# Moving the even steps' transposes in among the value products of an attention kernel, with all transposes in fp32r and one product made narrower

## The reference, cut to what matters

```python
h = _rmsnorm(x, norm_mix_g[l])
a_q, a_k, a_v, b_q, b_k, b_v, c_q, c_k, c_v, c_f, gates = jnp.split(h @ w_in[l], splits, axis=-1)
o_a = _diff_attention(...)           # 4 heads: (softmax(s0) - lam * softmax(s1)) @ v, v 128 wide
o_b = _chunk_band_attention(...)     # 8 heads of 64, own chunk of 64 keys and 8 before it
o_c = _forgetting_attention(...)     # 8 heads of 64, causal, with a cumulative log-forget bias
g = jax.nn.sigmoid(gates)
merged = g0 * (o_a @ w_br_a) + g1 * (o_b @ w_br_b) + g2 * (o_c @ w_br_c)
x = x + merged @ w_out[l]
h = _rmsnorm(x, norm_ffn_g[l])
x = x + (jax.nn.silu(gt) * up) @ w_down[l]
return _rmsnorm(x, final_norm_g)
```

## Time and profile before

| | |
|---|---|
| median of 3 runs | 1815.77 us (1815.49 to 1816.34) |
| profiled execution: time, span | 1817.18 us, 1815.4 us |
| PE busy | 1795.1 us (99% of the span), 9048 matmuls |
| PE weight loads busy | 1507.9 us (83%) |
| DVE, ACT, POOL busy | 1253.9 (69%), 898.9 (50%), 360.6 us (20%) |
| mean granted TensorE clock | 0.999 of full |

### The profile page before, as it was taken

How to read it: one execution, slowest core, us unless ns; L and a number is a source line. 1 busy time by engine, 2 the same in 40 slices (tenths; PEclk the granted TensorE clock), 3 DMA queues, 4 the chain that set the end, 5 groups by cost and what they waited for, 6 DMA issues and landing times. The chain is left out here.

```text
span 1815.4 us, 26104 instructions
## 1 busy us (share of the span) xinstructions
PE 1795.1 (99%) x9048; PEld 1507.9 (83%) x9048; DVE 1253.9 (69%) x2374; ACT 898.9 (50%) x1742; POOL 360.6 (20%) x350
## 2 busy tenths in 40 slices
PE   8999999999999999999999999999999999999998
PEld 6888888888888888888888888888888888888886
DVE  5467766666667775777646778787766877766665
ACT  5555655667666775743424224553333333344445
POOL 2356331212111121013310000003222232200011
PEclk9999999999999999999999999999999999999999
DMA  8526333322332233333336572226566576479522
GB/s 236 161 95 197 92 95 85 72 75 69 94 93 73 65 97 128 131 119 116 129 116 214 175 266 93 116 65 215 196 201 205 174 237 227 160 264 396 195 74 93
DMA packets 195945, 268.01 MB, mean 148 GB/s; under 512 B 9988, under 2 KB 132996, under 8 KB 191864
## 3 DMA queue, kind: packets, MB, share of 16 engines
q1 hardware_dynamic: 191944, 262.07, 43.9%
q0 software_dynamic: 1664, 4.19, 1.6%
q10 hardware_dynamic: 2224, 0.30, 0.1%
HBM read 187.82 MB, written 80.02 MB: 148 GB/s over the span
## 5 line engine op out<-in xcount | busy, mean ns | idle before, releaser
L220 PE MATMUL ps<-h_hi,w_hi 128*128 128x512 f32 x888 | 359.4, 405 | 3.9 <-DVE q_stack L1064 2.4
L222 PE MATMUL ps<-h_hi,w_lo 128*128 128x512 f32 x888 | 347.2, 391 | 0.0
L221 PE MATMUL ps<-h_lo,w_hi 128*128 128x512 f32 x888 | 346.6, 390 | 0.0
L857 POOL TENSOR_TENSOR w_lo<-w_raw,w_hi 128x256 fp32r<-128x256 f32 x148 | 109.7, 772 | 461.4 <-ACT w_hi L925 461.4
L222 PEld LDWEIGHTS ps<-h_hi,w_lo 128*128 128x128 f32 x888 | 166.7, 188 | 37.0
L220 PEld LDWEIGHTS ps<-h_hi,w_hi 128*128 128x128 f32 x888 | 166.5, 188 | 36.3 <-DVE q_stack L1064 3.2
L221 PEld LDWEIGHTS ps<-h_lo,w_hi 128*128 128x128 f32 x888 | 167.1, 188 | 29.1
L1093 DVE CUSTOM_DVE_ANT_0 probs_bc<-ps,bias 128x640 f32<-128x640 f32 (+7 forms) x128 | 90.5, 707 | 73.3 <-PE ps L1275 31.4
L2290 POOL TENSOR_TENSOR bias<-w_raw 128x512 f32<-128x512 f32 x19 | 26.9, 1414 | 521.6 <-DMA w_raw<-in_w_gate_up 509.4
L220 PE MATMUL ps<-down_ring_w,down_ring_a 128*128 128x512 f32 x308 | 119.8, 389 | 0.0
L221 PE MATMUL ps<-down_ring_w,down_ring_a 128*128 128x512 f32 x308 | 119.8, 389 | 0.0
(11 more groups left out here) (365 smaller groups left out, 4391.2 us busy)
## 6 DMA issues: line engine op xcount, KB each, us to landing
w_raw<-in_w_in SPq DMA_DIRECT2D x50, 512.0 KB, 5.3
w_raw<-in_w_gate_up SPq DMA_DIRECT2D x44, 512.0 KB, 4.3
k_stack<-k_stack SPq DMA_DIRECT2D x24, 512.0 KB, 5.4
gate_in<-gates_scratch SPq DMA_DIRECT2D x24, 512.0 KB, 3.7
down_rows<-in_w_down SPq DMA_DIRECT2D x11, 1024.0 KB, 7.0
hidden_scratch<-hidden_stage SPq DMA_DIRECT2D x22, 512.0 KB, 4.9
weight_sums_scratch<-weight_sums SPq DMA_DIRECT2D x11, 1024.0 KB, 4.9
gates_scratch<-gate_sigmoid SPq DMA_DIRECT2D x21, 512.0 KB, 3.1
```

The lines of the kernel that those rows point to most:

```text
L220: nc.tensor.matmul(out, w_hi, x_hi, start=first, stop=False)
L221: nc.tensor.matmul(out, w_hi, x_lo, start=False, stop=False)
L222: return nc.tensor.matmul(out, w_lo, x_hi, start=False, stop=last)
L857: last = nc.gpsimd.tensor_tensor(w_lo[part], w_raw[part], w_hi[part].bitcast(F32), ALU.subtract)
```

## The change

In branches 2 and 3, at even steps from 2 on, the transposes no longer stand as a burst between the scores and the pieces. The pieces come first, and then the products of the group, with one transpose put in after each high product and before its low product; transposes left over follow the last product. Odd steps and step 0 keep their order. In branch 1 the low product is 128 wide and no longer 256. The transposes of lines 535, 1964 and 2952 read their tiles as fp32r against the fp32r identity, and that identity is now made by GpSimd early in the first block and not by DVE later.

```diff
             pool.wait_ge(made, 3)
+            nc.gpsimd.tensor_copy(keep["ident_r"][:, :], ident[:, :]).then_inc(consts, 1)
             nc.gpsimd.memset(wf_both[:, :, :].bitcast(F32), 0.0).then_inc(made, 1)
...
-            dve.wait_ge(made, 3)
-            nc.vector.tensor_copy(keep["ident_r"][:, :], ident[:, :]).then_inc(consts, 1)
...
-                return nc.tensor.transpose(turn_bank(g)[:, j * P:(j + 1) * P],
-                                           x_all[:, 4 * half + j, k * P:(k + 1) * P], ident[:, :])
+                return nc.tensor.transpose(turn_bank(g)[:, j * P:(j + 1) * P].bitcast(F32R),
+                                           x_words[:, 4 * half + j, k * P:(k + 1) * P], keep["ident_r"][:, :])
...
-                        last = nc.tensor.matmul(pv_bank[:, 0:2 * P], pta_lo[:, lc % 4, x * P:(x + 1) * P], v,
+                        last = nc.tensor.matmul(pv_bank[:, 0:P], pta_lo[:, lc % 4, x * P:(x + 1) * P], v[:, 0:P],
                                                 start=False, stop=tile == n - 1)
...
-            def times_v_bc(b, c, g):
+            def times_v_bc(b, c, g, beside=None):
...
+                if beside is not None:
+                    pe.wait_ge(scaled[beside % 2], STEPS // 2 * (c["unit"] - UPB) + (beside // 2 + 1))
+                tiles = tiles_of(b, place_of(b, beside)[0])[1] if beside is not None else 0
...
+                    if tile < tiles:
+                        turn_tile(b, c, beside, tile)
+                        tile += 1
                     nc.tensor.matmul(pv_half(g)[0:HD, lo:hi], v[:, 0:HD], ptb_lo[:, m, k, lo:hi], start=False, stop=False)
                 last = nc.tensor.matmul(pv_half(g)[:, lo:hi], v, ptb_hi[:, m, k, lo:hi], start=False, stop=True)
                 last.then_inc(pv_group, 1)
+                for rest in range(tile, tiles):
+                    turn_tile(b, c, beside, rest)
+
+            def turn_tile(b, c, s, tile):
+                sizes = chunks_of(b, place_of(b, s)[0])
+                j = 0 if tile < sizes[0] else 1
+                lc, x = chunks_through(b, s - 1) + j, tile - sum(sizes[:j])
+                turn = nc.tensor.transpose(turn_bank[lc % 2][:, x * P:(x + 1) * P].bitcast(F32R),
+                                           probs_words[:, s % 3, tile * P:(tile + 1) * P], keep["ident_r"][:, :])
+                if x == sizes[j] - 1:
+                    turn.then_inc(turned, 1)
...
-                    if s in turns:
+                    if b == 0:
+                        if s in turns:
+                            turn_probs(b, c, s)
+                        next_pieces(pieces_at[s])
+                        if s >= 2 and s % 2 == 0:
+                            times_v_a(c, s // 2 - 1)
+                    elif s >= 2 and s % 2 == 0:
+                        next_pieces(pieces_at[s])
+                        times_v_bc(b, c, s // 2 - 1, s if s < STEPS else None)
+                    else:
                         turn_probs(b, c, s)
-                    next_pieces(pieces_at[s])
-                    if s >= 2 and s % 2 == 0:
-                        if b == 0:
-                            times_v_a(c, s // 2 - 1)
-                        else:
-                            times_v_bc(b, c, s // 2 - 1)
+                        next_pieces(pieces_at[s])
...
-                    last = nc.tensor.transpose(turn_view(t)[:, k, :], o_tile[:, t % 2, k * P:(k + 1) * P], ident[:, :])
+                    last = nc.tensor.transpose(turn_view(t)[:, k, :].bitcast(F32R), o_words[:, t % 2, k * P:(k + 1) * P],
+                                               keep["ident_r"][:, :])
...
-                        last = nc.tensor.transpose(turn_bank(g)[:, j * P:(j + 1) * P], normed[:, j, k * P:(k + 1) * P], ident[:, :])
+                        last = nc.tensor.transpose(turn_bank(g)[:, j * P:(j + 1) * P].bitcast(F32R),
+                                                   normed_words[:, j, k * P:(k + 1) * P], keep["ident_r"][:, :])
```

More of the change, by code:

```diff
@@ L233, in block_norm @@
         x_all = sb("x_all", [P, TT, D])
+        x_words = nc.alloc_sbuf_tensor_at("x_words", [P, TT, D], F32R, offset=113152)
         junk = sb("square_out", [P, 4, D])
@@ L592, in _ @@
             pe.wait_ge(scaled, 2)
+            pe.wait_ge(consts, 1)
             for j in range(2):
@@ L1305, in times_v_bc @@
                 close = both[-1] if len(both) > 1 else one[-1]
+                tile = 0
                 for k in [x for x in both + one if x != close] + [close]:
@@ L1441, in block_merge @@
         o_tile = h_hi_room[:, 1, :].rearrange("p (n f) -> p n f", n=2)
+        o_words = also("o_tile_words", [P, 2, BR_W], F32R, 6144)
         o_hi = [o_first_hi, keep["act_hi"], h_hi[:, KH:KT, :]]
@@ L2028, in block_ffn @@
         normed = merged[:, 0:4 * D].rearrange("p (t d) -> p t d", t=4)
+        normed_words = also("normed_words", [P, 4, D], F32R, 112640)
         junk = merged[:, 4 * D:6 * D].rearrange("p (t d) -> p t d", t=2)
```

## The result

The change makes the kernel slower: 1846.49 us in the median of 5 runs (1845.51 to 1847.82), against 1816.07 (1815.49 to 1816.34) before. The ratio is 1.0165, with an interval of 1.0154 to 1.0177. The profiled execution took 1846.5 us with a span of 1844.7, so the two spans differ by 29.3 us. The forecast was 1835, with a range of 1825 to 1845: the direction was right, the size too small and the time outside the range.

What follows compares the result with a forecast made beforehand. PE, busy for 99% of the span, was taken as the bound. Terms +12.7 (branch 2), +9.4 (branch 3), -1.1 and -1.7 sum to +19.3 us on the median of 1815.77, giving 1835 us, range 1825 to 1845.

Steps and rivals of the forecast that it cites:

- a rival with a chance of 0.03: Clock falls to half level for 3 us after eight long waits, each costing 1.5 us more: 1847 us; chance 0.03.
- g3 in branch 2: Steps 8 and 9: late transposes delay ACT's copy, exp and take-out, so PE goes on 2.0 us later per unit.
- g3 in branch 3: Steps 6 and 7: the same late chain costs PE 1.8 us per unit, 0.8 in the last unit.
- g4 in branch 2: Steps 12 and 13: ACT's copy of g4 comes late and PE, which did not wait before, loses 0.75 us per unit.
- Banks at steps 14 and 15: No scores between the two steps, so PE waits for both banks: 0.55 us per unit, 0.6 in branch 3.
- The price of an interleaved transpose: A transpose between a high and a low product costs 0.08 us, bounded by 0.06 and 0.135.
- What the interleaving gains by itself: Gain of 0.4 us per unit of branch 2, only 0.13 of it real, and nothing in branch 3.
- The narrow low product: Branch 1: 144 narrower low products gain between 0 and 8.6 us, taken as 0.0075 each, -1.1 us.
- fp32r: 160 transposes go from 0.109 to 0.085 us each: 4 us gain at most, 0 at least, taken as -1.7.
- the waits don't grow: Rival: ACT and DVE catch up inside the products, only gains are left, 1811.5 us; chance 0.05.
- transposes are dear: Rival: the low product pays like a 128-column load, 0.135 us, +9 us: 1844 and up; chance 0.09.
- only the g3 waits grow: Rival: bank and g4 waits are absorbed, 7 us less, 1828 us, inside the range; no chance of its own.

Runs made afterwards that it cites:

- the earlier take-out: Changed kernel with other take-out steps alone: g2 and g3 at steps 4 and 8 (branch 2), 4 and 6 (branch 3), g4 at 12: 1861.95 us.

## Why the prediction was wrong, and where it was right

**The step that failed is the clock, which the sum puts at nothing.** "Total: +12.7 + 9.4 - 1.1 - 1.7" takes the granted clock of 1.00 of the earlier trace rows as a constant, though it had been read in a stream without waits of 2 us, and leaves the half level to a rival with a chance of 0.03. The runs showed 10.5 us in its place: five stretches of 3.4 us at 0.50 in the branches, 1.5 us each and 7.5 together, at waits for g3 near 2 us, and one of 10.2 us in the first block, 3.0. Filling the waits without shortening them gave 7.4 us back in the seven units. The waits for g3 and their length the working had.

The rival had the mechanism right, in the branches, and its number, 1847 against 1846.49, by luck. It counted eight long waits and 12 us; the working itself has the last unit's at +0.8, so there are seven, and five of them brought the clock down in the profiled execution. The first block's 3.0, which no rival has, made up for part of the difference.

As to the first block, "The fp32 transposes ... 0 at least where the copies out of PSUM pace them" took 0 as the lower end of that gain. Paced transposes that get shorter leave PE emptier, and 10.2 us at 0.50 followed: the gain had a negative end.

The account, in spans: 29.3 in all, of it 10.5 for the clock. Everything else is 18.8, against a sum of 19.3 in the working. That the two lie so close is in part luck too, since terms that came out too large hide one that was missing. Part by part:

- *g3 in branch 2*, +2.0 predicted. From the start of step 8's scores to the pass at step 9 it is 6.54 us (320.75 to 327.29), where it was 4.74 (318.60 to 323.34): +1.8. Slightly too large; the working left out that the first pass behind the scores, with no burst before it, takes 0.07 less.
- *g3 in branch 3*, +1.8. The idle time before the pass at step 7 is 1.99, against 0.31 in the earlier trace rows: +1.7. Near enough.
- *g4 in branch 2*, +0.75. From the start of step 12's scores to the pass at step 13 it is 5.21 us (336.70 to 341.91), where it was 4.61 (331.19 to 335.80): +0.6. A little less than predicted.
- *Banks at steps 14 and 15*, +0.55 and +0.6. Restoring step 14 gave 0.47 a unit.
- *Not seen*: 0.70 of idle time before the products of step 6 in branch 2, 2.8 in the four units. Beside the clock it is what the sum lacked. There DVE's order is `project_low` of g2, the scores of step 7, low parts, and only then `o_out`, which frees PE's bank. PE's timeline, then DVE's, of the kernel after:

```profile
317.26 0.38 PE L1317 MATMUL ps<-probs_tb_hi,v_split 128*128 128x256 f32 x1 [0.70 <-DVE heads_out L1162]
```

```profile
315.21 0.69 DVE L1094 CUSTOM_DVE_ANT_0 probs_bc<-ps,bias 128x512 f32<-128x512 f32 x1
...
316.61 0.43 DVE L1162 TENSOR_TENSOR heads_out<-ps,o_low 64x256 f32<-64x256 f32 x1
```

- *The price of an interleaved transpose*, 0.08. It is 0.06 between two products 256 wide (322.84 to 322.90), and 0.08 to the next start beside a product 128 wide (323.38 to 323.46). My bounds held, and the value is near the lower one for most. By the rule of the Trainium skill ("TensorE: Matmul & The Clock Gate", LDWEIGHTS), columns / 1.2 ns, a load of 64 columns lasts an estimated 53 ns, and the slot would be about 0.06; at the wide products the trace agrees.
- *What the interleaving gains by itself*, 0.13 a unit and 0. Distances from start to start, added up over all transposes and products of a unit, come to 12.9 us in branch 2 and 15.3 in branch 3, both with most steps interleaved (old order at 8, 12, 14 and 6, 14) and with none. Only the pieces, which stand behind fewer bursts, get shorter, by 0.14 a unit in branch 2 and by nothing in branch 3. In branch 3 the scores take 0.8 more, 0.7 of it between the mask products and what follows them, where I had given 0.3; how much of that is waiting was not told apart.
- *The units altogether*: where no stretch fell, 58.8 against 55.25 in branch 2, +3.6 (3.2 predicted), and 62.6 against 60.3 in branch 3, +2.3 (2.6).
- *The narrow low product*, -1.1. Branch 1 is 0.8 shorter. PE's timeline of the kernel after, for the earlier trace rows:

```profile
252.50 0.28 PE L1292 MATMUL ps<-v_split,probs_ta_hi 128*128 128x256 f32 x1
252.62 0.22 PE L1294 MATMUL ps<-v_split,probs_ta_lo 128*128 128x128 f32 x1
252.68 0.39 PE L1247 MATMUL ps<-k_stack,q_stack 128*128 128x384 f32 x1
252.91 0.34 PE L1248 MATMUL ps<-k_stack,q_stack 128*128 128x384 f32 x1
```

The low product does give way after 0.06 and not 0.12, but the score behind it then takes 0.23 where the one after the earlier trace rows gave way after 0.18: most of it is paid one instruction later. Right in its size.
- *fp32r*, -1.7 in all. Behind the start of the last unit the old order with the other edits is 2.1 shorter than before. The first block shows no gain from it: with the clock up, the first unit starts at 71.8 with fp32r and filler, and at 71.7 to 72.1 with x in plain fp32.

Of the rivals, that the waits don't grow and that transposes are dear are both refuted; that only the g3 waits grow is refuted by step 14. (Its price was summed wrongly: the g4 and bank terms are 4 x 1.3 + 4 x 0.8 = 8.4 and not 7, which gives 1826.6 and not 1828.) Not settled: why five of the seven long waits brought the clock down and two, as long, did not; why fewer of the longer waits of the earlier take-out did; and whether the first block would fall with a wait of another length.

## What to carry to other kernels

Where a change puts new waits into a stream on PE that was dense, price the clock along with the wait: here each wait of 2 us that brought the half level cost 1.5 us more, and quicker transposes in a stretch that was paced by copies cost 3.0. A transpose moved behind other work costs by the chain that starts with it (copy, exponential, take-out), so follow that chain and each engine's fixed order to the next wait, and expect one that is taken away to come up again a step later. A slot between two products is worth little if the burst that it replaces costs 0.085 us a transpose and the slot 0.06 to 0.08.

## What the runs showed of the hardware that was not expected

- The granted clock fell to 0.50 for 3.4 us at five of seven waits of 2.0 to 2.2 us (start to start), in the kernel after and again in the one with x in plain fp32, but not at the same five, and at four of fourteen waits of 2.3 to 2.6 us in the one with the earlier take-out. In all three it fell between 0.3 us before the end of the wait and 1.3 us behind it. It did not fall at the seven waits of 1.7 to 1.8 us (start to start, 1.4 to 1.5 of idle time) with the burst behind the pieces, nor when PE worked through the 2 us.
- In the first block it fell for 10.2 us behind a wait of 1.44 and sixteen transposes paced by copies; the same transposes with filler between them stayed at 1.00. The Trainium skill ("TensorE: Matmul & The Clock Gate", "HAM oscillation — how this bites in real kernels") has idle gaps between groups of matmuls bring the clock down. The waits of this trace agree in kind, though the gaps that the page warns of are longer than the 2.0 to 2.2 us at which it fell here. In the first block the wait of 1.38 alone did not do it before the change; it also took shorter work.
- 15 superfluous products in each of eight places made a kernel 6.3 us faster (1846.49 to 1840.15).
